# One modulation slab of eight chunks, computed in the first down projection and not in the gated convolution's input

## What is computed

```
for i in 0, 1:
    sh1, sc1, g1, sh2, sc2, g2 = split(silu(c) @ w_ada[i] + b_ada[i], 6)
    h  = rmsnorm(x) * (1 + sc1) + sh1
    y  = differential attention(h, context)          if i == 0
         (gb * dwconv3(gc * xv)) @ w_out,  gb, gc, xv = split(h @ w_in, 3)   if i == 1
    x  = x + g1 * y
    h2 = rmsnorm(x) * (1 + sc2) + sh2
    x  = x + g2 * ((silu(g) * v) @ w_down),  g, v = split(dwconv3(h2 @ w_up), 2)
out = rmsnorm(x) * final_gain
```

## Time and profile before

| | |
|---|---|
| median of three runs | 2518.66 us (2515.16 to 2519.56) |
| the profiled execution | 2519.2 us, of it 2517.5 us span |
| PE busy | 2480.3 us, 99% of the span |
| DVE busy | 2054.5 us, 82% |
| ACT busy | 1259.0 us, 50% |
| POOL busy | 189.5 us, 8% |
| granted TensorE clock, mean | 0.996 |
| moved by DMA | 625.63 MB, mean 249 GB/s |
| `dn0` on PE | 1156.64 to 1401.91 us |
| `sin` on PE, after its first two slabs | 1426.80 to 1678.62 us |

### The profile page before, as it was taken

How to read it: one execution, slowest core, us unless ns; L and a number is a source line. 1 busy time by engine, 2 the same in 40 slices (tenths; PEclk the granted TensorE clock), 3 DMA queues, 4 the chain that set the end, 5 groups by cost and what they waited for, 6 DMA issues and landing times.

```text
span 2517.5 us, 37692 instructions
## 1 busy us (share of the span) xinstructions
PE 2480.3 (99%) x13562; PEld 2129.8 (85%) x13562; DVE 2054.5 (82%) x2723; ACT 1259.0 (50%) x1702; POOL 189.5 (8%) x282
## 2 busy tenths in 40 slices
PE   6999999999999999999999999999999999999998
PEld 4778888778988888888888988888988888888886
DVE  4888997899888889988888899989888877674554
ACT  5322334776655555555444544445655555554443
POOL 0002221000000001101111011101000000000000
PEclk9999999999999999999999999999999999999999
DMA  9768997556778779977988799978688766665554
GB/s 366 273 221 257 313 308 227 168 167 201 226 255 272 259 241 292 292 241 253 305 292 280 240 323 331 313 235 289 227 271 264 252 183 189 194 186 200 194 195 145
DMA packets 442704, 625.63 MB, mean 249 GB/s; under 512 B 18433, under 2 KB 358657, under 8 KB 435649
## 3 DMA queue, kind: packets, MB, share of 16 engines
q1 hardware_dynamic: 401904, 450.94, 54.6%
q0 software_dynamic: 40080, 172.25, 20.9%
q10 hardware_dynamic: 576, 0.48, 0.1%
HBM read 621.50 MB, written 2.10 MB: 248 GB/s over the span
## 4 chain that ended last, share of the span: by engine, by line
PE 87%; DVE 6%; DMA 4%; ACT 1%; issue 1%; SPq 1%; DVEq 0%; ACTq 0%
PE ps L2113 38%; PE ps L2121 20%; PE ps L2467 6%; PE ps L2136 5%; PE ps L2474 3%; DMA raw<-in_sconv_w_in_dram 3%; PE ps L2034 2%; PE ps L2143 2%; PE ps L2036 2%; PE ps L2035 2%; DVE w_lo L1202 2%; PE ps L2243 1%; DVE ada_sum L1272 1%; PE ps L2261 1%; DVE broad_sum L1340 1%
## 5 line engine op out<-in xcount | busy, mean ns | idle before, releaser
L662 ACT ACTIVATE w_hi<-raw 128x1024 fp32r<-128x1024 f32 (+1 forms) x792 | 821.9, 1047 | 860.8 <-PE ps L2121 257.8
L1202 DVE TENSOR_TENSOR w_lo<-raw,w_hi 128x1024 fp32r<-128x1024 f32 (+1 forms) x792 | 954.0, 1211 | 353.2 <-ACT w_hi L662 351.3
L2113 PE MATMUL ps<-both,w_hi 128*128 128x512 f32 x2944 | 698.0, 393 | 0.0
L2113 PEld LDWEIGHTS ps<-both,w_hi 128*128 128x128 f32 x2944 | 546.0, 188 | 115.7 <-issue 6.9
L2121 PEld LDWEIGHTS ps<-both,w_lo 128*128 128x128 f32 x2944 | 367.4, 191 | 9.6 <-issue 1.0
L2121 PE MATMUL ps<-both,w_lo 128*128 128x256 f32 x2944 | 371.5, 283 | 0.0
L1272 DVE SCALAR_TENSOR_TENSOR ada_sum<-ada_ring,vec,ada_sum 128x512 f32<-128x512 f32 x324 | 242.9, 750 | 11.9 <-DMA ada_ring<-in_w_ada_dram 4.6
L2467 PE MATMUL ps<-w_hi,act 128*128 128x512 f32 x704 | 175.2, 390 | 0.0
L2113 PE MATMUL ps<-xs_sin,w_hi 128*128 128x512 f32 x704 | 170.2, 393 | 2.5 <-ACT w_hi L662 2.1
L2113 PE MATMUL ps<-act,w_hi 128*128 128x512 f32 x704 | 164.8, 390 | 0.0
L2467 PEld LDWEIGHTS ps<-w_hi,act 128*128 128x128 f32 x704 | 131.5, 188 | 27.0
(11 more groups left out here) (258 smaller groups left out, 2895.6 us busy)
## 6 DMA issues: line engine op xcount, KB each, us to landing
raw<-in_ffn_w_up_dram SPq DMA_DIRECT2D x352, 512.0 KB, 4.6
ada_ring<-in_w_ada_dram POOLq DMA_DIRECT2D x176, 512.0 KB, 5.3
raw<-in_ffn_w_down_dram SPq DMA_DIRECT2D x152, 512.0 KB, 4.1
raw<-in_attn_w_qkv_dram SPq DMA_DIRECT2D x96, 512.0 KB, 4.9
broad_ring<-in_w_ada_dram POOLq DMA_DIRECT2D x48, 1024.0 KB, 6.1
raw<-in_sconv_w_in_dram SPq DMA_DIRECT2D x96, 512.0 KB, 5.8
ada_ring_kv<-in_w_ada_dram POOLq DMA_DIRECT2D x48, 512.0 KB, 5.3
raw<-in_attn_w_o_dram SPq DMA_DIRECT2D x32, 512.0 KB, 4.6
```

What stands on the lines that cost most here:

```text
L662: nc.scalar.activation(w_hi[:, slot, 0:n_tiles, :], raw[:, slot, 0:n_tiles, :], ACT.Copy).then_inc(hi_made, 1)
L1202: nc.vector.tensor_tensor(w_lo[:, slot, 0:n_tiles, :], raw[:, slot, 0:n_tiles, :], w_hi[:, slot, 0:n_tiles, :], ALU.subtract).then_inc(lo_ ...
L2113: last = mm(ps[:, bank + m, :], w_hi[:, slot, t, P * m:P * m + P], src[:, tile + t, :], start=(is_first and t == 0), stop=(is_last and t = ...
```

## The change

```diff
-SPREAD = {"up0": (13, 4, 15), "dn0": (17, 6, 15), "sin": (23, 3, 21)}
+SPREAD = {"up0": (13, 4, 15), "dn0": (17, 7, 12), "sin": (24, 2, 31)}
```

## The result

The changed kernel takes 2521.92 us (median of 20 runs, 2518.75 to 2526.26), the kernel before 2518.48 us, also over 20 runs: a ratio of 1.0016 with an interval of 1.0010 to 1.0022. It is **3.4 us slower**. The forecast was 2516.4 us, 2.1 us faster than before. The time lies within the range and within 0.2%, but on the other side.

The account below looks back on a forecast made before the run. PE was taken as the bound, busy 2480.3 of 2517.5 us, with 5.1 us of stalls in `sin` to win. -4.0 in `sin` and +1.2 in `dn0` made -2.8 against 2519.2: 2516.4 us, range 2513.3 to 2526.

Parts of the forecast that it names:

- What bounds the kernel, and the prize: Whole kernel: PE busy 2480.3 of 2517.5 us; three stalls of PE in `sin` bound the gain at 5.1 us.
- My term: `sin`: 4 of the 5.12 us lost to stalls taken as won, bounds 0 and 5.12.
- The reading of where chunks meet row blocks: `sin` after the change: a chunk still falls on the same unit as a row block at units 23 and 43.
- DVE's time alone stalls nothing: `dn0`: DVE goes from 26.2 to 29.0 of 31 us, 93%, which alone stalls nothing.
- DMA: `dn0`: traffic goes from 296 to about 323 GB/s, loads of `raw` from 5.4 towards 6.1 us, which fits.
- The rival in which POOL's queue takes half: `dn0`: `raw` gets 164 GB/s of the 188 asked, seven slabs take 247 us, total 2547; chance 0.03.
- The chunk ring: `dn0`: two slots, chunks hanging on ones three units before; DVE drifts behind, 1.2 us lost, bounds 0 and 24.
- The cycle of a slab: `dn0`: DVE needs 14.8 us for two ring turns plus 16.4, together 31.2 us, against PE's 30.66.
- The lead: `dn0`: DVE may fall back some 3 to 4 us before PE waits; the drift just about uses it up.
- chunk ring (slower): Rival in `dn0`: longer chunk landings make w_lo late and PE waits; 2525 at 6.3 us, 2532 at 6.8; chance 0.15.
- point of decision: `dn0`, slower ring rival: decides from a chunk landing of about 6.3 us, 32.6 us a slab, total 2525.
- What was to show it: Right: `dn0` has 10 to 20 DVE chunk waits of about 1 us; wrong: PE waits there over 3 us.

Follow-up runs that it names:

- the four runs that lose nothing in `dn0` and keep all loads: Changed kernel with half-column sums, 2514.76 us; with third slot from chunk 3 plus pairs, 2514.36; with that slot alone, 2514.26; kernel before with the slab in `up0`, 2514.35.
- The run with half the load: Changed kernel with half of the bytes of each `dn0` chunk loaded, DVE's instructions unchanged: 2513.88 us, ratio 0.9983.
- the last run with a third slot: Changed kernel with a third chunk slot in `dn0` used from chunk 3 on, PE's order unchanged: 2514.26 us, ratio 0.9983.
- the first one: Changed kernel with a third chunk slot in `dn0` used from chunk 2 on: 2516.55 us, ratio 0.9992.
- The run with pairs: Changed kernel with PE in `dn0` in the order high, high, low, low for each pair: 2519.12 us, ratio 1.0005.
- moving the slab to a stage with room: Kernel before with the extra slab given to `up0`, six slabs in `dn0` at the earlier pace and two in `sin`: 2514.35 us, ratio 0.9986.
- moving the fold: Changed kernel with all `dn0` chunks three units later, so the fold follows unit 1 of the next slab, not unit 10: 2527.18 us, ratio 1.0042.

## Why the prediction was wrong

**What bounds the kernel, and the prize: right.** The three stalls of `sin` are gone, and with them a wait of 0.39 us for `xs_sin` at 1434.79, which the prediction hadn't priced. The profile shows -5.84 us, more than the bound of 5.1. It is on the high side: the other profiles with three slabs in `sin` have 251.1 and 249.2 us there, and those with two 245.6 to 248.4. In the medians the prize is 3.7 us: the four runs that lose nothing in `dn0` and keep all loads stand at 2514.3 to 2514.8 us against 2518.0. My term was 4.0. (The reading of where chunks meet row blocks missed one: units 23, 43 and also 58. Nothing stalled there.)

**DVE's time alone stalls nothing: right.** The run with half the load has DVE at 92% and no wait. **DMA: right for the changed kernel.** `raw` in `dn0` went from 5.4 to 5.8 us, and even at 325 GB/s PE waited for nothing in the last run with a third slot; in the first one single loads of `raw` of 9 to 10 us did reach PE, by way of w_lo. The rival in which POOL's queue takes half didn't come: with `raw` at 188 GB/s asked, PE waited for no w_hi. Each queue's load slows the other's: the half load brought `raw` down from 5.8 to 4.5 us. The rule of the Trainium skill (DMA: Bandwidth & Descriptors, Queues, rings and completion order), that each DMA engine takes turns between its queues by packets, agrees with that direction; no run here shows the turns themselves.

**The chunk ring: the mechanism right, the size wrong.** This is the step that failed: *"DVE then falls back by 0.5 us a slab, 3.8 us over seven. It may fall back some 3 to 4 us before PE waits"*, and from it *"I take 1.2 us lost"*. By the medians the term is 2521.92 - 2514.26 = 7.7 us, by the profile 8.7. Two numbers in it were off, both the same way.

- *The cycle of a slab.* I had 31.2 us. From the first of PE's waits to the last are five slabs: (1376.30 - 1215.79) / 5 = 32.1 us, where PE alone needs 30.66. The table splits DVE's cycle as the prediction did, into the two turns of the ring, from the end of the chunk behind unit 4 to the end of the one behind unit 10, and the rest up to the next slab's unit 4. The last two columns are the landings of the two chunks that the turns wait for (us, read from the timelines of DVE and POOL, and from `ada_ring` at each issue).

| slab of `dn0` | rest ahead of it | two turns | landing, chunk behind unit 7 | landing, chunk behind unit 10 |
|---|---|---|---|---|
| predicted | 16.4 | 14.8 | 5.6 | 5.6 |
| 2 | 16.9 | 15.8 | 5.6 | 6.5 |
| 3 | 16.6 | 15.1 | 6.5 | 4.9 |
| 4 | 17.1 | 14.6 | 4.4 | 5.7 |
| 5 | 16.6 | 15.2 | 5.2 | 6.3 |
| 6 | 16.5 | 16.0 | 5.3 | 7.0 |
| 7 | 16.6 | 16.2 | 6.2 | 6.3 |

  Over the last five cycles the turns take 15.4 us in the mean and the rest 16.7. So of the 0.9 us by which I was short, some 0.6 lie in the turns and 0.3 in the rest (in slab 4 it has a late chunk behind unit 3). I took the median landing of all chunks, 5.6 us. The chunk behind unit 10, the one that hurts, had 6.3 us in the median of these six slabs. And a ring keeps what a late load costs and gives little back for an early one: in slab 4 a landing of 4.4 us, 1.2 less than my 5.6, shortened the turn by 0.3 us, as DVE had other work and came to that chunk only 5.6 us after the end of the one behind unit 4. The two turns of slab 6 (timeline of DVE, then POOL's issue and the landing of that chunk):

```profile
1323.57 1.53 DVE L1272 SCALAR_TENSOR_TENSOR ada_sum<-ada_ring,vec,ada_sum 128x512 f32<-128x512 f32 x2
...
1330.76 1.54 DVE L1272 SCALAR_TENSOR_TENSOR ada_sum<-ada_ring,vec,ada_sum 128x512 f32<-128x512 f32 x2
...
1339.61 1.54 DVE L1272 SCALAR_TENSOR_TENSOR ada_sum<-ada_ring,vec,ada_sum 128x512 f32<-128x512 f32 x2 [2.06 <-DMA ada_ring<-in_w_ada_dram]
```

```profile
1332.59 0.72 POOL L538 DMA_DIRECT2D ada_ring<-in_w_ada_dram  x1 [2.05 <-DVE ada_sum L1272]
```

```profile
DMA to landing us min/median/max: 7.0/7.0/7.0
```

- *The lead.* I took 3 to 4 us for seven slabs. The first wait of PE comes at the end of the second slab. The shortest lead counts, not the mean one: for the last w_lo of a three-tile group my own estimate gave 4.9 - 2.3 = 2.6 us. The kernel before bears it out, where DVE is as far ahead as the ring lets it (timeline of DVE, then of PE):

```profile
1333.32 0.96 DVE L1202 TENSOR_TENSOR w_lo<-raw,w_hi 128x768 fp32r<-128x768 f32 x1 [0.91 <-ACT w_hi L662]
```

```profile
1334.90 3.04 PE L2121 MATMUL ps<-act,w_lo 128*128 128x256 f32 x24
1337.77 6.54 PE L2113 MATMUL ps<-act,w_hi 128*128 128x512 f32 x28
```

  The w_lo of unit 11 is done at 1334.2, and the last six of the 24 low matmuls, which read it, begin at about 1337.05: 2.9 us. DVE in the first slab also still finishes `up0`, which may spend part of that; no run here separates it. The run with pairs shows the lead from the other side: an estimated 2.7 us more of it, and in its profile the first wait comes at the end of the sixth slab.

With 2.6 us of lead and 1.44 us a slab the loss is 7 x 1.44 - 2.6 = 7.5 us, about what was measured. That is no independent test, as the 1.44 is read from the same waits. The run with pairs is a better one: 2.7 us more of lead makes it 4.8 us, and by the medians it lost 2519.12 - 2514.26 = 4.9. The rival *chunk ring (slower)* was the mechanism that came; I gave it 0.15. I set its point of decision at a landing of 6.3 us for all chunks, and against it I held a median. The median of all didn't move, 5.6 us before and after, but that of the chunk behind unit 10 was at that very figure.

**What was to show it.** I named 10 to 20 waits of DVE of about 1 us behind units 7, 9 and 10: there were 18, 19.2 us. For a wrong forecast I named waits of PE of over 3 us, late in the stage: there were 7.0 us, through the stage from the second slab on.

## What to carry to other kernels

Before a prefetched stream is made denser, compare the time that its ring leaves between giving a slot back and needing it, at the tightest place of the schedule, with the whole spread of the landing times: where the wait stands in the queue of an engine that is nearly full, a third slot gave as much (2514.3 us) as moving the slab to a stage with room (2514.4), and more than moving the fold or changing PE's order. A full engine and a late load may each be harmless and stall the bound engine together, so halve one at a time before blaming either. And a lead is as long as its shortest place: the order in which the bound engine asks for its operands is part of it. Last, read a landing time at the place where it counts: the median of a whole stage hid the one chunk of each slab that set the pace.

## What the runs showed of the hardware that was not expected

Half of the bytes in a chunk brought its landing from 5.6 to 3.9 us and no further, so 256 KB beside the weight loads still take 70% of the time of 512 KB; and it took 1.3 us off the loads of another queue. PE was granted full clock through six idle stretches of up to 1.94 us in `dn0` (the window from 1156 to 1402, which has all six, says 1.00), while in the kernel before the one of 2.09 us in `sin` stands in a window at 0.95.
